# 88 gathered tokens in place of 80, key scores in quads between the query groups, and 16-bit look-up tables in the sort

## What is computed

```
def chunk(hc):                                   # hc: 128 tokens x 1024
    q = (hc @ wq).reshape(T, 8, 2, 128)          # 8 heads, 2 halves
    s1 = einsum('thd,hnd->thn', q[:, :, 0], sub_keys[:, 0])   # 128 keys
    s2 = einsum('thd,hnd->thn', q[:, :, 1], sub_keys[:, 1])
    v1, i1 = top_k(s1, 16);  v2, i2 = top_k(s2, 16)
    cand = v1[..., :, None] + v2[..., None, :]   # 16 x 16 sums per head
    sc, ci = top_k(cand, 16)
    e = take(i1, ci // 16) * 128 + take(i2, ci % 16)   # of 16384 experts
    g = softmax(sc)
    act = gelu(einsum('td,thkd->thk', hc, exp_u[e]))
    return einsum('thk,thkd->td', g * act, exp_v[e])
x = x + g2 * peer(h2);  return rmsnorm(x, final_g)
```

## Time and profile before

| | us |
|---|---|
| median of 3 runs (858.42, 861.15, 862.43) | 861.15 |
| the profiled execution's own time | 859.74 |
| its span, first to last instruction | 857.9 |
| PE busy | 833.6 (97%) |
| DVE busy | 548.3 (64%) |
| POOL busy | 198.4 (23%) |
| ACT busy | 172.7 (20%) |
| moved by the DMA engines | 277.94 MB, mean 324 GB/s |

### The profile page before, as it was taken

One profiled execution on the slowest core, in us unless ns is written; L12 is line 12 of the kernel. 1 busy time (PEld: TensorE's weight loads), 2 busy tenths in 40 slices (PEclk: granted clock), 3 DMA queues, 4 the chain that ended last, 5 costly groups with the idle time before them and its releaser, 6 DMA issues.

```text
span 857.9 us, 14450 instructions
## 1 busy us (share of the span) xinstructions
PE 833.6 (97%) x5758; PEld 806.1 (94%) x5758; DVE 548.3 (64%) x1113; ACT 172.7 (20%) x452; POOL 198.4 (23%) x201
## 2 busy tenths in 40 slices
PE   6999999999999999999999999999999999999996
PEld 4998879889999999999999999989999999999996
DVE  5859889755998998678788887743344445342002
ACT  5464585523111112111111111000000000000003
POOL 2000000000103333633343435433333233231000
PEclk9999999999999999999999999999999999999998
DMA  9998791702878998999999999999999999999771
GB/s 337 402 386 319 306 395 47 313 6 79 234 244 301 388 392 270 406 408 408 368 350 353 358 364 361 406 410 370 408 392 402 379 399 410 384 373 315 222 234 58
DMA packets 72644, 277.94 MB, mean 324 GB/s; under 512 B 8225, under 2 KB 10513, under 8 KB 71298
## 3 DMA queue, kind: packets, MB, share of 16 engines
q1 hardware_dynamic: 48626, 191.52, 59.1%
q0 software_dynamic: 23952, 85.50, 26.8%
HBM read 275.50 MB, written 1.49 MB: 323 GB/s over the span
## 4 chain that ended last, share of the span: by engine, by line
PE 90%; DVE 4%; DMA 3%; ACT 1%; issue 1%; another core or an unknown queue 1%; SPq 0%; ACTq 0%; DVEq 0%
PE banks L1218 35%; PE banks L1189 34%; PE banks L925 3%; PE banks L858 3%; PE banks L1201 2%; PE banks L878 2%; PE banks L921 2%; DMA raw<-in_v_b 1%; PE banks L863 1%; DMA raw<-in_u_t 1%; PE banks L994 1%; DVE sc_w L1328 1%; PE banks L834 1%; PE banks L1178 1%; PE banks L894 1%; PE banks L1083 1%
## 5 line engine op out<-in xcount | busy, mean ns | idle before, releaser
L1189 PE MATMUL banks<-hT,raw 128*128 128x176 f32 x2048 | 311.3, 313 | 1.8 <-DMA raw<-in_u_t 1.5
L1218 PE MATMUL banks<-act,raw 128*128 128x176 f32 x2048 | 308.8, 313 | 1.7 <-DMA raw<-in_v_b 1.7
L1218 PEld LDWEIGHTS banks<-act,raw 128*128 128x128 f32 x2048 | 305.6, 190 | 3.6 <-DMA raw<-in_v_b 3.5
L1189 PEld LDWEIGHTS banks<-hT,raw 128*128 128x128 f32 x2048 | 305.5, 190 | 2.5 <-DMA raw<-in_u_t 2.0
L1652 DVE SCALAR_TENSOR_TENSOR sum_pair<-rows,weight,sum_pair 128x1024 f32<-128x1024 f32 x63 | 80.9, 1285 | 103.9 <-DMA rows<-in_v_b,idx 103.0
L541 POOL DMA_INDIRECT rows<-in_v_b,idx x80 | 90.4, 1130 | 174.0 <-PE banks L1218 129.2
L541 POOL DMA_INDIRECT rows<-in_u_rows,idx x80 | 95.4, 1192 | 138.9 <-DVE dots L1630 120.8
L1630 DVE CUSTOM_DVE_ANT_0 rows<-rows,h_pair 128x1024 f32<-128x1024 f32 x64 | 77.2, 1222 | 8.9 <-DMA rows<-in_u_rows,idx 4.6
L790 ACT ACTIVATE turned<-banks,g_col 128x256 f32<-128x256 f32 x8 | 3.8, 473 | 307.5 <-PE banks L1218 307.5
L748 ACT ACTIVATE act<-banks 128x176 f32<-128x176 f32 (+21 forms) x123 | 34.1, 277 | 125.2 <-PE banks L1189 120.4
L505 POOL DMA_DIRECT2D h_lines<-h_stage x1 | 0.5, 527 | 209.5 <-ACT h_stage L773 209.5
(11 more groups left out here) (248 smaller groups left out, 862.8 us busy)
## 6 DMA issues: line engine op xcount, KB each, us to landing
raw<-in_u_t SPq DMA_DIRECT2D x128, 512.0 KB
raw<-in_v_b SPq DMA_DIRECT2D x128, 512.0 KB
wq<-in_wq SPq DMA_DIRECT2D x2, 4096.0 KB, 18.0
sh_w<-in_w_mod SPq DMA_DIRECT2D x8, 512.0 KB, 12.5
sc_w<-in_w_mod SPq DMA_DIRECT2D x8, 512.0 KB, 13.5
win<-in_w_in SPq DMA_DIRECT2D x8, 512.0 KB, 14.2
win<-in_w_in SPq DMA_DIRECT2D x1, 4096.0 KB, 20.9
sc_w<-in_w_mod SPq DMA_DIRECT2D x2, 2048.0 KB, 23.1
```

The source lines that it names most:

```text
L1189: last = nc.tensor.matmul(dst, raw[n % RAW][:, c * P:(c + 1) * P], hT[:, c, 0:MANY], start=(c == 0), stop=(c == DC - 1))
L1218: return nc.tensor.matmul(chunk_place(c)[:, 0:MANY], raw[(BLOCKS + j) % RAW][:, c * P:(c + 1) * P], act[:, j, :], start=(j == 0 and c < 4) ...
```

## The change

- FEW goes from 80 to 88: kinds of 64, 16 and 8 tokens (a third kind with 16 partitions a token), 176 gathers in all. MANY goes from 176 to 168, so 21 gate groups in place of 22; `few_sums` has a third matmul per chunk.
- The key scores are computed in four quads of lists, after the query groups 2, 4, 6 and 7 (`key_scores`, `keep_scores`), into banks 0 and 1. `score` and the sort's tables lie elsewhere so that the sort of t=1 can begin between the query groups (`sort_quads`).
- The chunks for `g2` are loaded ahead of the first blocks, through the ring's buffers, and reduced by DVE among the query groups (`second_gate`); `crow2` and its way through DRAM are gone, `crow` is used.
- `top_i`, `part`, `hit` and the compared places (`place_h`) are 16-bit floats.
- The ring has 6 buffers, the early gathers 6 slots in place of 4. Gathers 23 to 87 of U also wait for the block count (PACE_U). EXP_AT 49 to 50, GATE_AT 59 to 60.

```diff
-RAW = 5
-PAIRED = 64
-SPREAD = 16
-FEW = PAIRED + SPREAD
+RAW = 6
+GATE_RAW = 5
+KINDS = (64, 16, 8)
+FEW = sum(KINDS)
-EARLY_SLOTS = 4
+EARLY_SLOTS = 6
-EXP_AT = 49
+EXP_AT = 50
-GATE_AT = 59
+GATE_AT = 60
+PACE_U = 1.0
...
-        hit = at("hit", R[3] + 6144, [P, HEADS, TOPK, TOPK])
+        hit = at("hit", R[3] + 6144, [P, HEADS, TOPK, TOPK], F16)
...
+        QUAD_AFTER = (2, 4, 6, 7)
...
         def s_bank(g):
-            return (6, 7, 2, 3)[g % 4]
+            return g % 2
...
+            for c in range(DC):
+                if c >= GATE_RAW:
+                    sp.wait_ge(sc2_read, DC + c - GATE_RAW + 1)
+                sp.dma_start(raw[c % GATE_RAW][:, :], w_mod[4][:, c, :]).then_inc(shift_in[c], 16)
             for n in range(STREAM):
+                if n < RAW:
+                    sp.wait_ge(sc2_read, DC + (n + 1 + GATE_RAW if n + GATE_RAW < DC else n + 1 if n < GATE_RAW else DC))
                 if n >= RAW:
                     sp.wait_ge(block_used, n - RAW + 1)
...
-                if n == BLOCKS + ROW_LOAD:
-                    sp.wait_ge(lines_moved, LINE_SAVED)
-                    sp.dma_start(crow2[:, :], c_lines.ap().broadcast_to([P, D])).then_inc(crow2_in, 16)
-                since = n - BLOCKS - G2_LOAD
-                if 0 <= since < 8 * DC and since % 8 == 0:
-                    c = since // 8
-                    sp.dma_start(g2_w[:, c, :], w_mod[4][:, c, :]).then_inc(shift_in[c], 16)
...
-            for k in range(P // PAIRED):
-                pool.dma_start(h2_pair[k * PAIRED:(k + 1) * PAIRED, :], ...)
-            pool.dma_start(h2_spread[:, :], ...)
+            for n, count in enumerate(KINDS):
+                pool.dma_start(h2_rows[n][:, :],
+                               bass.AP(tensor=h2_lines, offset=KIND_AT[n] * D, ap=[[0, P // count], [D, count], [1, D]])
+                               ).then_inc(lines_moved, 16)
...
+                if EARLY + 4 < i < TILES:
+                    pool.wait_ge(block_used, TURN_AT + int((i - EARLY - 4) * PACE_U))
...
+            def key_scores(f):
+                if f == 0:
+                    pe.wait_ge(loaded["keys"], 16)
+                    pe.wait_ge(proj_out, N_IN + 2)
+                else:
+                    pe.wait_ge(q_sum, 2 * f)
+                    pe.wait_ge(s_out, 2 * f)
+                for g in range(2 * f, 2 * f + 2):
+                    t = 1 - g % 2
+                    for l in range(4 * f, 4 * f + 4):
+                        last = nc.tensor.matmul(bank[s_bank(g)][:, l % 4 * P:(l % 4 + 1) * P],
+                                                qT[:, l, t * P:(t + 1) * P], keys[:, l, :], start=True, stop=True)
+                    last.then_inc(s_ready, 1)
...
                 for c in range(DC):
-                    nc.tensor.matmul(... sum_pair[:, cols], fold_pair[:, :] ...)
-                    nc.tensor.matmul(... sum_spread[:, cols], fold_spread[:, :] ...)
+                    for n in range(len(KINDS)):
+                        nc.tensor.matmul(chunk_place(c)[:, MANY + KIND_AT[n]:MANY + KIND_AT[n + 1]],
+                                         row_sums[n][:, c * P:(c + 1) * P], folds[n][:, :], start=False, stop=False,
+                                         skip_group_check=True)
...
+            GATE_CHUNKS = {2: (0, 1, 2), 3: (3,), 4: (4, 5), 5: (6, 7)}
             for g in range(LISTS // 2):
                 for e in range(2):
                     low_part(WQ + g, (e, e + 1), weights_low)
                 if g >= 3:
                     query_sum(g - 1)
+                for c in GATE_CHUNKS.get(g, ()):
+                    second_gate(c)
...
+                sort_quads({6: 2, 7: 4}.get(g, 0))
             query_sum(LISTS // 2 - 1)
+            sort_quads(LISTS // 4 * 5 - quad_steps[0])
```

More of the change, by code:

```diff
@@ L35 @@
 STREAM = 2 * BLOCKS
-RAW = 5
-PAIRED = 64
-SPREAD = 16
-FEW = PAIRED + SPREAD
+RAW = 6
+GATE_RAW = 5
+KINDS = (64, 16, 8)
+FEW = sum(KINDS)
 MANY = SEQ - FEW
 FEW0 = P - FEW
-TILES = PAIRED + SPREAD
+TILES = FEW
+KIND_AT = [sum(KINDS[:n]) for n in range(len(KINDS) + 1)]
 GATHERS = 2 * TILES
-EARLY_SLOTS = 4
+EARLY_SLOTS = 6
 EARLY = 18
@@ L63 @@
 GATE_SCALE = 2.0 ** 14
-ROW_LOAD = 14
-G2_LOAD = 24
-G2_SUM = 32
 AHEAD = 10
 PACE = 1.45
+PACE_U = 1.0
 BEFORE_GATES = 4
@@ L728, in _ @@
                     high_group(WQ + g + 3)
+                if g in QUAD_AFTER:
+                    keep_scores(QUAD_AFTER.index(g))
             warm_table(0, ACT.Gelu)
[L731 to L735 removed]
             def gelu(n):
@@ L1168, in _ @@
                 query_wide(WQ + g, g)
-            pe.wait_ge(loaded["keys"], 16)
-            for g in range(TT * LISTS // 4):
-                t, four = 1 - g % 2, g // 2
-                if g in (0, 6):
-                    pe.wait_ge(q_sum, LISTS // 2 - 3 if g == 0 else LISTS // 2 - 2)
-                if g >= 4:
-                    pe.wait_ge(s_out, g - 3)
-                for e in range(4):
-                    l = 4 * four + e
-                    last = nc.tensor.matmul(bank[s_bank(g)][:, e * P:(e + 1) * P], qT[:, l, t * P:(t + 1) * P],
-                                            keys[:, l, :], start=True, stop=True)
-                last.then_inc(s_ready, 1)
+                if g in QUAD_AFTER:
+                    key_scores(QUAD_AFTER.index(g))
             def u_block(n):
@@ L1602, in query_sum, with second_gate, top16_step, top16 @@
                                         ALU.add).then_inc(q_sum, 1)
+            def second_gate(c):
+                ve.wait_ge(shift_in[c], 32)
+                w = raw[c % GATE_RAW]
+                nc.vector.tensor_tensor_reduce(out=w[:, :], in0=w[:, :], in1=crow[:, :], scale=1.0,
+                                               scalar=bcol[:, 4, c:c + 1], op0=ALU.mult, op1=ALU.add,
+                                               accum_out=g2_col[:, c:c + 1]).then_inc(sc2_read, 1)
+            def top16_step(vals, pos, src, lists, step):
+                k = step // 3 * 8
+                for l in lists:
+                    if step % 3 == 0:
+                        last = nc.vector.max(vals[:, l, k:k + 8], src(l))
+                    elif step % 3 == 1:
+                        last = nc.vector.max_index(pos[:, l, k:k + 8], vals[:, l, k:k + 8], src(l))
+                    else:
+                        last = nc.vector.match_replace(src(l), vals[:, l, k:k + 8], src(l), -3.0e38)
+                link(last)
+            def top16(vals, pos, src, n, between):
+                for step in range(5):
+                    top16_step(vals, pos, src, range(n), step)
+                    between()
+            GATE_CHUNKS = {2: (0, 1, 2), 3: (3,), 4: (4, 5), 5: (6, 7)}
+            quad_steps = [0]
+            def sort_quads(n):
+                for _ in range(n):
+                    f, step = quad_steps[0] // 5, quad_steps[0] % 5
+                    if step == 0:
+                        ve.wait_ge(s_out, 2 * f + 1)
+                    top16_step(top_v, top_iu, lambda l: score[:, 1, l, :], range(4 * f, 4 * f + 4), step)
+                    quad_steps[0] += 1
             for g in range(LISTS // 2):
@@ L1656, in weights @@
             def weights(n):
-                cols = slice(0, PAIRED) if n == 0 else slice(PAIRED, TILES)
+                cols = slice(KIND_AT[n], KIND_AT[n + 1])
                 ve.wait_ge(lines_moved, FEW_IN)
```

182 lines of the change are left out of this document (74 added, 108 removed).

## The result

The changed kernel takes 846.19 us (median of 4 runs, 844.74 to 849.66), the kernel before 861.79 us in the same series (4 runs, 858.42 to 863.12). The ratio is 0.9828, with a 95% interval of 0.9801 to 0.9856: 15.6 us less, where 26 were forecast. The direction was right, the size was not, and 846.2 lies above the range.

What follows compares the result with a forecast made beforehand. PE was taken to set the time, with the DMA engines as the next wall. The terms summed to -26.1 us, taking 859.74 to 833.6, or 835.0 by the median; it said 835, range 829 to 843.

Steps and rivals of the forecast that it cites:

- term 1: U and V dense passes: 4096 passes narrow from 176 to 168 columns, 6.7 ns less each, -27.4 us.
- rivals A: Gate stage: DVE becomes the bound, the period stays at 8.13 us, +7.6 us, giving 842; chance 0.10.
- E: U and V passes: no shorter, since loading 128 weight columns sets the pace; about 862 us; chance 0.03.
- Term 3: Last quad of key scores, behind query group 7: PE waits for that group's sum and two hand-overs, +1.4 us.
- Term 4: Query groups: `g2` chunks reduced there stand ahead of the low part of group 3, +0.3 us.
- term 6: V stage: the stall with the `crow2` load goes, -1.7 us; second gate group: ACT's stall may go, -0.6 us.
- The cover in the sort: Sort, up to PE turning the tables at block 55: DVE about 9 us ahead of PE, no stall.
- the tables are hidden: Sort: 16-bit tables cost and give PE nothing; the four multiplications of `hit` save DVE 4.2 us.
- the paragraph on the wall of the DMA engines: V and gate stages: demand, 389 GB/s in V, stays inside the 398 and 409 GB/s the trace carried.
- Rival D: From block 55 on: transfers decide, engines full at 355 GB/s against 394 wanted, +52 us, giving 887; chance 0.03.
- Term 2: Folds (`few_sums`): the third kind adds 8 small matmuls with nothing beside them, +1.8 us.
- Term 5: Front: slow reads of repeated h2 lines, 1.5 MB after 1 MB, starve the ring, +1.0 us, ends -1.5 and +4.

Runs made afterwards that it cites:

- Folds in sixes: Changed kernel with the 24 small folding matmuls spread over V blocks 116 to 123, three behind each, instead of one run; 844.46 us, ratio 0.9811.
- with eighty tokens: Changed kernel with kinds (64, 16) again, 176 dense columns, everything else of the change kept; 856.40 us, ratio 0.9949.
- the kernel with the later lines: Changed kernel with 1 of 1.5 MB of repeated h2 lines read behind gathers 30 and 36, not before the first; 849.42 us, ratio 0.9866.

## Why the prediction was wrong

**Right.** What a pass is worth (term 1): 0.1427 us, 6.5 ns less than 0.1492 where 6.7 were taken. In the gate stage three blocks and a group fell from 8.13 to 7.81 us (6.89 + 0.92), and the stage by 10.4 us where 9.3 were forecast; rivals A (DVE bound) and E (weight loads set the pace) are out. Term 3: PE waited 1.5 us for the last sum, 1.4 forecast. Term 4: PE waited 0.2 us for the low parts, 0.3 forecast. The stall at the second gate group (term 6) is gone. The cover in the sort held, by 3.63 us, and the tables are hidden, as said. A mix of 409 GB/s was carried with PE at full pace in the gate stage, so the trace of before was the right judge there. The 358 GB/s of the Trainium skill that the prediction names did not bind: the gate stage moved 388 GB/s and the V stage 381.

**The step that failed** is the paragraph on the wall of the DMA engines, and through it the V share of term 1. It divided the bytes of a V block by its time, 389 GB/s, found it below 398 and 409, and stopped. But a queue shares by what stands in it, not by its mean. With the head start of ten falling into the first V blocks, the gathers had work at every moment; the two full queues got 205 GB/s each, and a block took 2.55 us whatever the mean says, until the backlog was gone after 47 blocks. The rows at 409 GB/s with a full PE, on which the paragraph leaned, were from the gate stage, where a block and its third of a group took 2.71 us before (8.13/3) and take 2.60 now (7.81/3): longer than the 2.56 of half the rate, so that sharing costs nothing there. They could not vouch for blocks of 2.28 us. The excess over 1984 passes at 0.1427 (283.1) is 10.5 us; before, the like excess was 3.4 (299.4 less 296.0), of which 1.7 was PE's wait for a V block. The kernel before had this period too: in the window of 535.4 to 620 us of the earlier trace rows, PE was busy 82.92 of 84.60 us. I read that as full pace with one stall; it was also a short stretch of the same sharing. From 561.66 to 578.78 us PEld took up a block every 2.56 us (the row at 564.21 above), but for one gap of 4.33 us, the stall, behind the `crow2` load that SP had issued at 559.75. Rival D had the right resource, but with a wrong trigger (the mean, below 373 GB/s) and a price of 52 us, where 9 were lost. The runs with four other pairs of head start and pace show the cause; the release of the gathers was not part of the priced change, since its numbers had not been edited, but their moment moved: U's last gather went from 513.2 to 521.9 us.

**Term 2 was mis-sized.** It took +1.8 for the folds and nothing behind them. Measured is +2.6, and +2.4 over the forecast in the rest of the kernel. A folding pass at the full clock even cost less than forecast (4.6 us for 48, where 5.3 were taken); the clock's fall was not in the sum. Folds in sixes bring back 1.5 and 2.3 us at these two places. Nothing in the trace of before showed it, as 32 such passes leave the clock at 1.00.

**Term 5** was low, though inside its ends. PE's waits on U blocks are 3.1 us where before there were 1.5, and PEld stood idle for 4.7 us of the first 55 blocks where it was 2.1. The stage lost 2.8 us against the bare passes (880 x 6.7 ns = 5.9, measured -3.1), where +1.0 stood in the sum. That the expert lines also landed late did no harm, since DVE had 3.6 us in hand. **Term 6** was low: with eighty tokens the V stage went from 299.4 to 296.0 us, 3.4 in place of 1.7, as the sharing at V's start was absorbed too (there the ring has one block more, and `crow2` and the `g2` chunks are gone; which of these did it wasn't parted). The start of U came 0.5 us later than terms 3 and 4 say; that is left open.

## What to carry to other kernels

When two queues feed one engine, don't only compare the mean demand with the rate that was carried: ask whether the second queue has a backlog. Here the first then got half, and the loss was (blocks until the backlog was gone, less some 9 that the ring still covered) x (half-rate period less compute period). A faster consumer has the shorter compute period and so loses more per block: 0.27 us here, 0.16 at eighty tokens. Release the secondary stream evenly over the stage, and count again when a change shifts the moment at which its head start falls. Small matmuls that are added to a run of small ones can cost more than their own time; put them between wide ones.

## What the runs showed of the hardware that was not expected

- With the blocks' queue and the gathers' queue both full, each moved its half: 8.91 and 8.23 MB in 42 us, 409 GB/s together, held for 118 us.
- TensorE's clock fell to 1.2 GHz while PE was busy without a gap (3.00 of 3.00 us in each window). The Trainium skill, page "TensorE: Matmul & The Clock Gate", part 1, section "What's actually happening", says that the throttled state is the default and activity releases it. The trace has both sides: in the kernel with the later lines the clock was 0.84 from 390 to 400 us, after PE had been busy for only 5.85 of 10 us, but at the end of the changed kernel it fell though PE's record has no gap. What PE did there was a run of 48 folding passes of 8 to 64 columns, with the fall inside it; with 32 in a row, and with 48 in sixes, it stayed at 1.00.
- In 16-bit floats a compare of which one operand repeats along the innermost axis and a reduction took the same 2.29 us as in 32 bits, a plain multiplication 1.22.
- Lines repeated from few rows cost more where the DMA engines had no slack: 1 MB in the gate stage gave PE 5.2 us of waits, 1.5 MB at the front 3.1.
